# Eight of 22 feature tiles of the last down projection as seven block products, in three of its four output pairs

## The chip, the cores and the metric

The kernel runs on one core of one Trainium2 chip. The metric is the device time of one execution in microseconds (us): 1068.31, the median of three runs (1067.3 to 1068.74).

## What is computed

Two layers over 512 frames of 1024 features in float32. Layer 0 mixes tokens by latent attention, layer 1 by a gated short convolution, and each layer ends in the same feed-forward block; a last RMSNorm closes the trunk:

```python
for i in range(DEPTH):                                   # DEPTH = 2
    h = h + (mla_mixer if i % 2 == 0 else short_conv_mixer)(rms_norm(h, ...), ...)
    h = h + swiglu(rms_norm(h, ffn_norm[i]), ffn_w_gate[i], ffn_w_up[i], ffn_w_down[i])
return rms_norm(h, final_norm)

def swiglu(h, w_gate, w_up, w_down):                     # (512,1024) -> (512,2816) -> (512,1024)
    return (jax.nn.silu(h @ w_gate) * (h @ w_up)) @ w_down
```

The change is in the last product of all, `... @ w_down` of layer 1, and in the residual addition and norm behind it.

## The kernel before

Features lie on the 128 partitions, the 512 frames along the free dimension. So the residual stream is eight tiles of 128x512 (`xT`, "head" in the profile, since it shares that buffer), and the inner activations of the feed-forward block are 22 tiles (`inner`). A float32 product is made of three TensorE matmuls (lines 466 to 468): both operands are split into a high part rounded to `fp32r` and a rest, and high x high, high x rest and rest x high are added in a PSUM bank.

Weights stream in chunks through two slots. For each chunk the DMA queue loads `raw[s]`, ScalarE writes the high parts (`split`, L897), VectorE writes the rests (`split`, L1347), and then TensorE may read the slot. The semaphores are `raw_loaded`, `hi_split`, `w_split` and, when TensorE has read the last of a chunk, `chunk_done`; ScalarE waits for `chunk_done` before it overwrites the high parts. Each engine runs its own list in the written order. There is no scheduler: the order of the Python statements in the engine's block is the order on the engine.

The gate and up products use a seven-product block scheme, `winograd`: a pair of feature tiles and a pair of output tiles are taken as 2x2 blocks, and instead of eight block products there are seven, on 256 columns each, plus sums of blocks. The sums of the weights are made by VectorE in `forms` (four additions of 128x512) and split like a chunk (`forms_split`: 128x2048, then 128x1536 for the sums); the sums of the activations by `x_forms` (four subtractions of 128x256 for each pair of tiles). Between the products ScalarE copies partial sums out of the banks (L1173, L1180), and VectorE adds the four corners of the result.

The down projection is plain before the change. Eight output tiles are made in four pairs, and each pair takes its 22 feature tiles in three chunks, of 8, 8 and 6 tiles (`DOWN_K`). The first pair starts while the last inner tiles are still being split: ScalarE makes `inner_hi`, VectorE `inner_lo` (`inner_rests`, L1390), and TensorE waits for each tile by `operand_ready`. In `ffn` of VectorE the tail of this is: the rests of tiles 5 to 11, the split of the second weight chunk, the rests of tiles 12 to 21, and then, in `down_round`, the split of the third chunk. Of the last pair the second output tile is computed in two halves of 256 frames (`last_pair`), so that the norm can begin on the first half. Each finished tile is scaled by `rstd` and added to the residual (`add_scaled`), ScalarE squares it and VectorE adds the squares; `weigh` multiplies by the gains of the final norm, and the tail transposes, scales and stores.

`DOWN_AHEAD` gives the sizes of the chunks that are split ahead. `DOWN_BANKS` are the PSUM banks: (4, 5) and (6, 7); `HALF_BANKS` (7, 3) the two halves of the last tile.

## Time and profile before

| | |
|---|---|
| median of 3 runs | 1068.31 us |
| profiled execution, its own time | 1069.4 us |
| its span, first to last instruction | 1067.6 us |
| TensorE busy | 1057.6 us, 99% of the span |
| TensorE weight load busy | 956.1 us |
| VectorE busy | 806.5 us, 76% |
| ScalarE busy | 507.1 us, 48% |
| granted TensorE clock, mean | 1.000 |

A busy time is a sum over a whole engine. Matmuls overlap in the record: a 512-column matmul is listed with 0.39 us, but the next one starts 0.23 us later, so it is the distance from start to start that counts. "PEld" is the loading of the stationary operand, which overlaps too.

### The profile page before, as it was taken

What the parts mean: (1) busy time and instruction counts of PE and PEld (TensorE: products, weight loads), DVE (VectorE), ACT (ScalarE), POOL (GpSimd) and SP (SyncE); (2) the same over time, 40 slices, a digit from 0 to 9 for tenths busy, and PEclk for the clock granted to TensorE, in tenths of its full rate; (3) what the DMA queues carried; (4) which work ended last, traced back from release to release, by engine and by line L of the source; (5) the groups of instructions that cost most, each with busy time, mean ns of one, the idle gap of its engine ahead of it and who ended that gap; (6) DMA issues with size and microseconds to landing.
All of it is one profiled execution on the core that took longest, in us unless ns stands there. A gap on an engine that the chain in (4) does not pass through costs nothing.

```text
span 1067.6 us, 17579 instructions
## 1 busy us (share of the span) xinstructions
PE 1057.6 (99%) x6714; PEld 956.1 (90%) x6714; DVE 806.5 (76%) x1133; ACT 507.1 (48%) x720; POOL 40.5 (4%) x22
## 2 busy tenths in 40 slices
PE   9999999999999999999999999999999999999998
PEld 7788888889999999888888888888999999988887
DVE  5767774999999998734578677689999999873343
ACT  6586664745545555521353323365545554651221
POOL 0232221000000000000000000000000000000000
PEclk9999999999999999999999999999999999999999
DMA  7311121223233233233223232222333233222212
GB/s 270 116 63 40 56 79 45 114 99 103 113 118 115 82 117 108 80 108 108 93 95 107 91 115 83 91 107 80 118 118 112 87 115 118 97 91 108 99 40 80
DMA packets 16966, 106.21 MB, mean 99 GB/s; under 512 B 1888, under 2 KB 2272, under 8 KB 6432
## 3 DMA queue, kind: packets, MB, share of 16 engines
q1 hardware_dynamic: 16848, 105.43, 27.5%
q8 instruction: 25, 0.41, 0.2%
q0 software_dynamic: 80, 0.26, 0.1%
q14 instruction: 13, 0.11, 0.0%
HBM read 103.59 MB, written 2.10 MB: 99 GB/s over the span
## 4 chain that ended last, share of the span: by engine, by line
PE 91%; DVE 1%; ACT 1%; issue 1%; DVEq 0%
PE bank L466 30%; PE bank L468 29%; PE bank L467 29%; PE bank L613 1%; PE bank L627 1%; ACT split L1163 1%; DVE s_lo L1703 0%; PE bank L505 0%; PE bank L615 0%; PE bank L851 0%; PE bank L863 0%; DVE work L1692 0%; DVE raw L1690 0%; DVE sq L1397 0%; DVE work L1687 0%
## 5 line engine op out<-in xcount | busy, mean ns | idle before, releaser
L466 PE MATMUL bank<-x_hi,split 128*128 128x256 f32 (+1 forms) x704 | 204.4, 290 | 0.0
L467 PE MATMUL bank<-x_lo,split 128*128 128x256 f32 (+1 forms) x704 | 203.6, 289 | 0.0
L468 PE MATMUL bank<-x_hi,split 128*128 128x256 f32 (+1 forms) x704 | 203.6, 289 | 0.0
L897 ACT ACTIVATE split<-raw 128x2048 fp32r<-128x2048 f32 (+2 forms) x54 | 95.8, 1774 | 184.4 <-PE bank L468 180.4
L1347 DVE TENSOR_TENSOR split<-raw,split 128x2048 fp32r<-128x2048 f32 (+2 forms) x46 | 99.4, 2161 | 98.2 <-ACT split L897 98.1
L467 PE MATMUL bank<-inner_lo,split 128*128 128x512 f32 (+1 forms) x374 | 140.9, 377 | 0.0
L466 PE MATMUL bank<-inner_hi,split 128*128 128x512 f32 (+1 forms) x374 | 140.9, 377 | 0.0
L468 PE MATMUL bank<-inner_hi,split 128*128 128x512 f32 (+1 forms) x374 | 140.8, 376 | 0.0
L466 PE MATMUL bank<-x_hi,s_hi 128*128 128x256 f32 x480 | 134.4, 280 | 0.6 <-ACT work L1173 0.6
L467 PEld LDWEIGHTS bank<-x_lo,split 128*128 128x128 f32 x704 | 132.3, 188 | 3.0 <-issue 0.5
L466 PEld LDWEIGHTS bank<-x_hi,split 128*128 128x128 f32 x704 | 132.3, 188 | 3.0 <-issue 0.5
L468 PEld LDWEIGHTS bank<-x_hi,split 128*128 128x128 f32 x704 | 132.3, 188 | 2.5
L467 PE MATMUL bank<-x_lo,s_hi 128*128 128x256 f32 x480 | 134.0, 279 | 0.0
L468 PE MATMUL bank<-x_hi,s_lo 128*128 128x256 f32 x480 | 134.0, 279 | 0.0
L1697 DVE TENSOR_TENSOR split<-raw,split 128x2048 fp32r<-128x2048 f32 x44 | 100.8, 2290 | 14.8 <-ACT split L1163 13.2
L1163 ACT ACTIVATE split<-raw 128x2048 fp32r<-128x2048 f32 x44 | 84.3, 1915 | 43.0 <-DVE work L1692 42.9
L466 PE MATMUL bank<-a_hi,split 128*128 128x512 f32 (+1 forms) x264 | 100.9, 382 | 1.7 <-DVE split L1347 1.0
L468 PE MATMUL bank<-a_hi,split 128*128 128x512 f32 (+1 forms) x264 | 99.4, 377 | 0.0
L467 PE MATMUL bank<-a_lo,split 128*128 128x512 f32 (+1 forms) x264 | 99.4, 376 | 0.0
L1180 ACT ACTIVATE work<-bank 128x256 f32<-128x256 f32 x44 | 16.9, 385 | 164.0 <-PE bank L468 164.0
L466 PEld LDWEIGHTS bank<-x_hi,s_hi 128*128 128x128 f32 x480 | 90.2, 188 | 1.3 <-ACT work L1173 1.0
L467 PEld LDWEIGHTS bank<-x_lo,s_hi 128*128 128x128 f32 x480 | 90.2, 188 | 0.0
(240 smaller groups left out, 2087.3 us busy)
## 6 DMA issues: line engine op xcount, KB each, us to landing
raw<-weights_in SPq DMA_DIRECT2D x82, 1024.0 KB, 4.8
raw<-weights_in SPq DMA_DIRECT2D x12, 768.0 KB, 4.3
work<-x SPq DMA_DIRECT2D x4, 512.0 KB, 11.4
raw<-weights_in SPq DMA_DIRECT2D x4, 512.0 KB, 3.8
out<-head SPq DMA_DIRECT2D x3, 512.0 KB, 3.1
head<-head_in SPq DMA_DIRECT2D x1, 768.0 KB, 9.0
raw<-weights_in SPq DMA_DIRECT2D x3, 192.0 KB, 3.9
raw<-weights_in SPq DMA_DIRECT2D x1, 576.0 KB, 7.6
```

Of the source, the lines that this page charges most:

```text
L466: pe.matmul(o, lhs[0], rhs[0], start=start, stop=False, skip_group_check=True)
L467: pe.matmul(o, lhs[0], rhs[1], start=False, stop=False, skip_group_check=True)
L468: return pe.matmul(o, lhs[1], rhs[0], start=False, stop=stop, skip_group_check=True)
L613: pe.matmul(o, qr, key, start=False, stop=False, skip_group_check=True)
L627: tr = pe.transpose(bank[b][:, j * P:(j + 1) * P], work[:, p0:p0 + P], ident[:, :])
L897: act.activation(w_hi[s][:, 0:n], raw[s][:, 0:n], ACT.Copy).then_inc(hi_split[s], 1)
L1163: act.activation(block_hi[s][:, :], raw[s][:, :], ACT.Copy).then_inc(hi_split[s], 1)
L1180: act.activation(copies[g][0], bank[b][:, 0:HT], ACT.Copy).then_inc(drained[b], 1)
L1347: v.tensor_tensor(w_lo[s][:, 0:n], raw[s][:, 0:n], w_hi[s][:, 0:n], ALU.subtract).then_inc(w_split[s], 1)
L1697: v.tensor_tensor(block_lo[s][:, :], raw[s][:, :], block_hi[s][:, :], ALU.subtract).then_inc(w_split[s], 1)
```

## The change

1. The chunks of layer 1's down projection are cut 8, 6, 8 instead of 8, 8, 6 (`LAST_K`), and the pairs take them in the order of `LAST_ORDER`; the order of the loads (`LAST_N`) follows.
2. For output pairs 1, 2 and 3 the chunk of the last eight feature tiles (14 to 21) is computed by `winograd` from sums of the weights and of the activations. Pair 0 stays plain.
3. The sums of the activations are new work: `inner_forms` (VectorE, four subtractions of 128x256 for each of four pairs of tiles), their high parts (ScalarE) and their rests (`inner_tail_rest`). They are placed in the space of the gate and up operands, which are dead by then.
4. The block products end in banks 0 to 3 and not in the banks that hold the other 14 tiles' sum. So their corners are put together (`down_corners`), scaled and added to the residual on their own (`add_corners`), and the sum of the 14 tiles is added apart (`pair_sums`).
5. The last pair is ordered 8 tiles, block product, 6 tiles; within a chunk the whole tile is now done ahead of both halves (`last_pair`), and the second half uses bank 5 instead of 3.
6. ScalarE's load of the square-root table (`idle_sqrt`) moves from the middle of the projection to a place after the last copies of the last block product.

The core of the diff:

```diff
+LAST_K = [range(0, 8), range(8, 14), range(14, KF)]
+LAST_ORDER = [(0, 1, 2)] * 2 + [(0, 2, 1)] * 2
+LAST_N = [len(LAST_K[i]) * 2 * P for order in LAST_ORDER for i in order]
...
-LEFT_BANKS, HALF_BANKS = (4, 5, 7, 6), (7, 3)
+LEFT_BANKS, HALF_BANKS = (4, 5, 7, 6), (7, 5)
...
                 if last:
-                    for c in range(6):
-                        down_chunk(c)
-                    for c in range(3):
-                        down_chunk(c)
-                    for c in range(3, 6):
-                        last_pair(c)
+                    banks = DOWN_BANKS[0]
+                    chunk(0, banks, INNER, LAST_K[0], True, False, ready=made)
+                    chunk(1, banks, INNER, LAST_K[1], False, False, ready=made)
+                    last_tiles(0, banks, LAST_K[2], made)
+                    chunk(1, DOWN_BANKS[1], INNER, LAST_K[0], True, False)
+                    last_tiles(0, DOWN_BANKS[1], LAST_K[1])
+                    pe.wait_ge(inner_split, K_PAIRS)
+                    winograd(1, 0, inner_block, DOWN_SUMS)
+                    chunk(0, banks, INNER, LAST_K[0], True, False)
+                    winograd(1, 0, inner_block, DOWN_SUMS)
+                    last_tiles(0, banks, LAST_K[1])
+                    last_pair(1, DOWN_BANKS[1][0], LAST_K[0], False)
+                    winograd(0, 0, inner_block, DOWN_SUMS)
+                    last_pair(1, DOWN_BANKS[1][0], LAST_K[1], True)
...
+            def last_tiles(s, banks, ks, ready=None):
                 pe.wait_ge(w_split[s], T.add(f"slot{s}"))
+                for m, b in enumerate(banks):
                     for n, k in enumerate(ks):
+                        if ready is not None and m == 0:
+                            pe.wait_ge(operand_ready, ready + k + 1)
+                        mm = product(bank[b][:, :], slot(s, (n * 2 + m) * P), operand(INNER, k), False, n == len(ks) - 1)
+                    mm.then_inc((tile_summed, chunk_done[s])[m], 1)
...
+            def down_copies_of(s):                        # ScalarE
+                for n in (1, 5, 6):
+                    down_copy(n)
+                act.wait_ge(chunk_done[s], T.now(f"slot{s}"))
+                act.activation(down_copies["last"], bank[0][:, 0:HT], ACT.Copy).then_inc(drained[0], 1)
...
+            def inner_forms(k, m):                        # VectorE
+                (b11, b12), (b21, b22) = (tuple(half_of(tile(inner, m + i), h) for h in range(2)) for i in range(2))
+                t1, t2, t3, t4 = (inner_tail[:, k * 2 * SEQ + n * HT:k * 2 * SEQ + (n + 1) * HT] for n in range(4))
+                taken()
+                taken()
+                do(v.tensor_tensor(t1, b12, b11, ALU.subtract))
+                do(v.tensor_tensor(t3, b22, b12, ALU.subtract))
+                settle()
+                do(v.tensor_tensor(t2, b22, t1, ALU.subtract))
+                settle()
+                v.tensor_tensor(t4, b21, t2, ALU.subtract).then_inc(inner_formed, 1)
+                v.wait_ge(inner_formed, k + 1)
+                for i in range(m, m + 2):
+                    ready(lo(tile(inner_lo, i), tile(inner, i), tile(inner_hi, i)))
...
-                split(1)
-                inner_rests(range(12, KF))
+                split(1, DOWN_N[1] if name else LAST_N[1])
+                if name:
+                    inner_rests(range(12, KF))
+                else:
+                    inner_rests(range(12, LAST_K[2][0]))
+                    for k in range(K_PAIRS):
+                        inner_forms(k, LAST_K[2][2 * k])
...
+                def last_down():                          # VectorE
+                    split(0)
+                    split(1)
+                    for k in range(K_PAIRS):
+                        inner_tail_rest(k)
+                    pair_sums(DOWN_BANKS[0], (0, 1), 0, True)
+                    split(0, LAST_N[1])
+                    added()
+                    add_squares([tile(work, 4), tile(work, 5)])
+                    forms(1)
+                    forms_split(1, DOWN_SUMS)
+                    pair_sums(DOWN_BANKS[1], (2, 3), 0, False)
+                    settle()
+                    split(0)
+                    v.wait_ge(sums_split[1], T.now("sums1"))
+                    forms(1)
+                    down_corners(1)
+                    forms_split(1, DOWN_SUMS)
+                    add_corners((2, 3), True)
...
+                    down_corners(0)
+                    add_corners((KD - 2, KD - 1), False)
+                    settle()
+                    v.wait_ge(tile_summed, T.add("summed"))
+                    add_scaled(DOWN_BANKS[1][0], KD - 2)
```

Where it moves instructions. First VectorE, between the last gate and up products and the down projection; `split0` and `split1` are the weight slots, `inner_57` the inner tiles, and a row is one instruction (or several alike). Before, from the rests of tile 5 on:

```order
L1390 TENSOR_TENSOR inner_lo_58<-inner_57,inner_hi_59 128x512 [waits hi_taken,step]
L1390 TENSOR_TENSOR inner_lo_58<-inner_57,inner_hi_59 128x512 [waits hi_taken] x6
L1347 TENSOR_TENSOR split1<-raw1,split1 128x2048 [waits hi_split1]
L1390 TENSOR_TENSOR inner_lo_58<-inner_57,inner_hi_59 128x512 [waits hi_taken] x10
L1347 TENSOR_TENSOR split0<-raw0,split0 128x1536 [waits hi_split0]
L1347 TENSOR_TENSOR split1<-raw1,split1 128x2048 [waits hi_split1]
```

After, from the same place (the last rows are the first of four such groups):

```order
L1472 TENSOR_TENSOR inner_lo_58<-inner_57,inner_hi_59 128x512 [waits hi_taken,step]
L1472 TENSOR_TENSOR inner_lo_58<-inner_57,inner_hi_59 128x512 [waits hi_taken] x6
L1429 TENSOR_TENSOR split1<-raw1,split1 128x1536 [waits hi_split1]
L1472 TENSOR_TENSOR inner_lo_58<-inner_57,inner_hi_59 128x512 [waits hi_taken] x2
L1884 TENSOR_TENSOR inner_tail_80<-inner_57 128x256 [waits hi_taken]
L1885 TENSOR_TENSOR inner_tail_80<-inner_57 128x256
L1887 TENSOR_TENSOR inner_tail_80<-inner_57,inner_tail_80 128x256 [waits step]
L1889 TENSOR_TENSOR inner_tail_80<-inner_57,inner_tail_80 128x256 [waits step]
L1472 TENSOR_TENSOR inner_lo_58<-inner_57,inner_hi_59 128x512 [waits inner_formed]
L1472 TENSOR_TENSOR inner_lo_58<-inner_57,inner_hi_59 128x512
```

The rests of the last eight tiles are now made in four groups of two, each behind four subtractions. Second, VectorE from the fourth of these groups on, after:

```order
L1884 TENSOR_TENSOR inner_tail_80<-inner_57 128x256 [waits hi_taken]
L1885 TENSOR_TENSOR inner_tail_80<-inner_57 128x256
L1887 TENSOR_TENSOR inner_tail_80<-inner_57,inner_tail_80 128x256 [waits step]
L1889 TENSOR_TENSOR inner_tail_80<-inner_57,inner_tail_80 128x256 [waits step]
L1472 TENSOR_TENSOR inner_lo_58<-inner_57,inner_hi_59 128x512 [waits inner_formed]
L1472 TENSOR_TENSOR inner_lo_58<-inner_57,inner_hi_59 128x512
L1429 TENSOR_TENSOR split0<-raw0,split0 128x2048 [waits hi_split0]
L1429 TENSOR_TENSOR split1<-raw1,split1 128x2048 [waits hi_split1]
L1898 TENSOR_TENSOR inner_tail_lo_81<-inner_tail_80,inner_tail_hi_79 128x1024 [waits inner_tail_high] x4
L1942 TENSOR_TENSOR work<-bank4,rstd 128x512 [waits squares_added,tile_summed]
```

Only behind the fourth group stands the split of slot 0, which the third chunk of the first pair needs; before, it stood behind the plain rests. On TensorE the wait for it (`w_split0`) has moved ahead by two feature tiles, or 12 matmuls of 512 columns: it was at feature tile 16 and is at 14. Third, TensorE in the last output pair. Before, the whole tile (bank 6) and the two halves (banks 7 and 3) are interleaved:

```order
L466 MATMUL bank6<-inner_hi_59,split0 128x512
L467 MATMUL bank6<-inner_lo_58,split0 128x512
L468 MATMUL bank6<-inner_hi_59,split0 128x512
L466 MATMUL bank7<-inner_hi_59,split0 128x256
L467 MATMUL bank7<-inner_lo_58,split0 128x256
L468 MATMUL bank7<-inner_hi_59,split0 128x256
L466 MATMUL bank3<-inner_hi_59,split0 128x256
L467 MATMUL bank3<-inner_lo_58,split0 128x256
L468 MATMUL bank3<-inner_hi_59,split0 128x256
L466 MATMUL bank6<-inner_hi_59,split1 128x512 [waits w_split1]
```

After, the last half matmuls of the first chunk (bank 5) are followed by the block product in banks 0 to 3, which waits for these banks and for slot 0:

```order
L479 MATMUL bank5<-inner_hi_59,split1 128x256
L480 MATMUL bank5<-inner_lo_58,split1 128x256
L481 MATMUL bank5<-inner_hi_59,split1 128x256
L479 MATMUL bank0<-inner_hi_59,split0 128x256 [waits drained2,drained1,drained3,drained0,w_split0]
L480 MATMUL bank0<-inner_lo_58,split0 128x256
L481 MATMUL bank0<-inner_hi_59,split0 128x256
L479 MATMUL bank0<-inner_hi_59,split0 128x256
```

## Rows read from the trace of the kernel before

**Rows 1.** The page, busy time, share of the span, instructions of each engine.

```profile
PE 1057.6 (99%) x6714; PEld 956.1 (90%) x6714; DVE 806.5 (76%) x1133; ACT 507.1 (48%) x720; POOL 40.5 (4%) x22
```

**Rows 2.** The page, the chain that ended last, by engine.

```profile
PE 91%; DVE 1%; ACT 1%; issue 1%; DVEq 0%
```

**Rows 3.** Waits of TensorE: waited for, us in total, times, longest.

```profile
PE bank L466 <- DVE split L1347: 1.4, 2, 1.0
```

**Rows 4.** Busy time by engine in one stretch: PE, PEld, DVE, ACT, POOL.

```profile
966.00:1026.00 60.00, 60.00 (x266) 49.71 (x265) 20.64 (x18) 14.25 (x12) 0.00 (x0) 1.00 0.27 98
```

**Rows 5.** Timeline of TensorE in the down projection: start, duration, instruction.

```profile
936.27 0.40 PE L466 MATMUL bank<-inner_hi,split 128*128 128x512 f32 x1
...
1026.04 0.39 PE L466 MATMUL bank<-inner_hi,split 128*128 128x512 f32 x1
...
1048.53 0.40 PE L466 MATMUL bank<-inner_hi,split 128*128 128x512 f32 x1
...
1052.64 0.28 PE L466 MATMUL bank<-inner_hi,split 128*128 128x256 f32 x1
...
1056.83 0.28 PE L468 MATMUL bank<-inner_hi,split 128*128 128x256 f32 x1
```

**Rows 6.** Timeline of ScalarE: last copies of two consecutive block products.

```profile
916.93 0.38 ACT L1180 ACTIVATE work<-bank 128x256 f32<-128x256 f32 x1 [3.88 <-PE bank L468]
...
926.73 0.38 ACT L1180 ACTIVATE work<-bank 128x256 f32<-128x256 f32 x1 [3.88 <-PE bank L468]
```

**Rows 7.** Timeline of VectorE at the start of the down projection.

```profile
939.07 4.30 DVE L1390 TENSOR_TENSOR inner_lo<-inner,inner_hi 128x512 fp32r<-128x512 f32 x7
943.29 2.28 DVE L1347 TENSOR_TENSOR split<-raw,split 128x2048 fp32r<-128x2048 f32 x1
945.49 6.10 DVE L1390 TENSOR_TENSOR inner_lo<-inner,inner_hi 128x512 fp32r<-128x512 f32 x10
951.51 1.75 DVE L1347 TENSOR_TENSOR split<-raw,split 128x1536 fp32r<-128x1536 f32 x1
960.25 2.29 DVE L1347 TENSOR_TENSOR split<-raw,split 128x2048 fp32r<-128x2048 f32 x1 [6.99 <-ACT split L897]
```

**Rows 8.** Timeline of VectorE: four block subtractions of the convolution's operands, the next instruction.

```profile
554.68 0.42 DVE L1644 TENSOR_TENSOR conv_form<-conv_form 128x256 f32<-128x256 f32 x1
...
555.47 0.43 DVE L1647 TENSOR_TENSOR conv_form<-conv_form 128x256 f32<-128x256 f32 x1
555.93 0.42 DVE L1649 TENSOR_TENSOR conv_form<-conv_form 128x256 f32<-128x256 f32 x1
556.27 0.68 DVE L1687 TENSOR_TENSOR work<-raw 128x512 f32<-128x512 f32 x1
```

**Rows 9.** Timeline, VectorE and TensorE: the longest wait for a split.

```profile
21.98 2.29 DVE L1347 TENSOR_TENSOR split<-raw,split 128x2048 fp32r<-128x2048 f32 x1 [2.38 <-ACT split L897]
...
24.32 0.50 PE L466 MATMUL bank<-a_hi,split 128*128 128x512 f32 x1 [0.95 <-DVE split L1347]
```

**Rows 10.** Timeline of ScalarE at the start of the down projection.

```profile
942.27 5.31 ACT L911 ACTIVATE inner_hi<-inner 128x512 fp32r<-128x512 f32 x10
...
958.30 1.92 ACT L897 ACTIVATE split<-raw 128x2048 fp32r<-128x2048 f32 x1 [9.34 <-PE bank L468]
```

**Rows 11.** Timeline of TensorE: its last matmuls.

```profile
1061.49 1.04 PE L872 MATMUL bank<-ident,raw 128*128 128x128 f32 x8
```

**Rows 12.** Stretches at the end: PE busy, granted clock (here 0.20 us each).

```profile
1066.60:1066.80 0.20, 0.00 (x0) 1.00 0.09 31
1066.80:1067.00 0.20, 0.00 (x0) 0.55 0.00 0
```

**Rows 13.** Stretches at the start: PE busy and its matmuls (x), granted clock.

```profile
2.00:3.00 1.00, 1.00 (x7) 1.00 0.88 151
...
5.00:6.00 1.00, 1.00 (x10) 1.00 0.79 228
```

**Rows 14.** Timeline of VectorE: the scaling of the last whole tile.

```profile
1052.84 0.69 DVE L1612 TENSOR_TENSOR work<-bank,rstd 128x512 f32<-128x512 f32 x1 [11.10 <-PE bank L468]
```

More of the change, by code:

```diff
@@ new lines, in whole, with half, last_pair @@
+            def whole(s, b, n, k):
+                return product(bank[b][:, :], slot(s, n * 2 * P), operand(INNER, k), k == 0, False)
+            def half(s, h, n, k):
+                return product(bank[HALF_BANKS[h]][:, 0:HT], slot(s, (n * 2 + 1) * P),
+                               tuple(half_of(t, h) for t in operand(INNER, k)), k == 0, False)
+            def last_pair(s, b, ks, ends):
+                pe.wait_ge(w_split[s], T.add(f"slot{s}"))
+                if ks[0] == 0:
+                    open_bank(b)
@@ new lines, in pair_sums @@
+            def pair_sums(banks, ms, s, final):
+                for b, m in zip(banks, ms):
+                    if b == banks[0]:
+                        v.wait_ge(tile_summed, T.add("summed"))
+                    else:
+                        done(s)
+                    t = tile(work, 4 + b % 2)
+                    v.wait_ge(squares_added, T.now("added"))
+                    drain(b, v.tensor_tensor(t, bank[b][:, :], rstd[:, :], ALU.mult))
+                    landed(b)
+                    add_to_x(t, m, final)
@@ L1829, in down_round @@
                             add_scaled(banks[0], ms[0])
-                            if last and pair == 1:
-                                added()
-                                weigh([ms[0]])
-                                add_squares([tile(work, 4)])
-                            if last and pair == 1:
-                                continue
                             done(c % 2)
@@ L1838, in down_round @@
                             next_operands(ms, name)
-                        if not (last and c >= 4):
-                            split(c % 2, DOWN_AHEAD[c])
-                        if name and m:
+                        split(c % 2, DOWN_AHEAD[c])
+                        if m:
                             conv_operands(c)
-                        if last and c in (2, 3):
-                            v.wait_ge(w_split[c % 2], T.now(f"slot{c % 2}"))
-                        if last and c == 2:
-                            weigh(range(KD // 2))
@@ L1847, in down_round, with last_down @@
-                        if last and c == 3:
-                            weigh(range(KD // 2, KD - 2))
-                down_round(0, False)
-                down_round(4, not name)
+                def last_down():
+                    split(0)
+                    split(1)
+                    for k in range(K_PAIRS):
+                        inner_tail_rest(k)
+                    pair_sums(DOWN_BANKS[0], (0, 1), 0, True)
+                    split(0, LAST_N[1])
+                    added()
[3 more added lines that the diff above has]
+                    pair_sums(DOWN_BANKS[1], (2, 3), 0, False)
+                    settle()
+                    split(0)
+                    v.wait_ge(sums_split[1], T.now("sums1"))
[3 more added lines that the diff above has]
+                    add_corners((2, 3), True)
+                    added()
+                    add_squares([tile(work, 4), tile(work, 5)])
+                    split(0, LAST_N[1])
+                    down_corners(1)
+                    split(1)
+                    add_corners((4, 5), False)
+                    settle()
+                    forms(0)
+                    pair_sums(DOWN_BANKS[0], (4, 5), 0, True)
+                    forms_split(0, DOWN_SUMS)
+                    added()
+                    add_squares([tile(work, 4), tile(work, 5)])
+                    v.wait_ge(w_split[0], T.now("slot0"))
+                    v.wait_ge(sums_split[0], T.now("sums0"))
+                    weigh(range(KD // 2))
+                    split(1, LAST_N[1])
+                    v.wait_ge(w_split[1], T.now("slot1"))
+                    weigh(range(KD // 2, KD - 2))
+                    down_corners(0)
+                    add_corners((KD - 2, KD - 1), False)
+                    settle()
+                    v.wait_ge(tile_summed, T.add("summed"))
+                    add_scaled(DOWN_BANKS[1][0], KD - 2)
+                    added()
+                    weigh([KD - 2])
+                    add_squares([tile(work, 4)])
@@ L2016, in weight_stream @@
         for m in range(KD // 2):
-            for ks in DOWN_K:
-                yield columns(w["ffn_w_down"][layer][ks[0] * P:(ks[-1] + 1) * P], span(m * 2 * P))
+            for i in LAST_ORDER[m] if layer else range(3):
+                ks = (LAST_K if layer else DOWN_K)[i]
+                chunk = columns(w["ffn_w_down"][layer][ks[0] * P:(ks[-1] + 1) * P], span(m * 2 * P))
+                yield block_order(chunk) if layer and m and i == 2 else chunk
 def kernel(**inputs):
```

140 lines of the change are left out of this document (101 added, 39 removed).

## The prediction, made before the changed kernel had run

> **What bounds the kernel now.** I read the page first. TensorE is busy in 99% of the span [rows 1], and the chain that ended last lies on it for 91% [rows 2]. The waits come next: in the whole execution TensorE waits for a weight split for 1.4 us [rows 3]. In its middle TensorE is busy without a break for 60 us while VectorE works 20.6 us and ScalarE 14.3 us of them [rows 4]. So what counts there is the number of matmuls and their distance from start to start, and whatever makes TensorE wait is added in full. The start of this stage is different. There VectorE works without a break from 939.07 to 953.26 [rows 7], since TensorE has begun the projection at 936.27 [rows 5] while the rests of the inner tiles are still being made.
>
> **What TensorE saves.** A 512-column matmul costs the distance of its start to the next. Three output pairs are 3 x 132 = 396 of them, from 936.27 to 1026.04 [rows 5]: 0.2267 us each. A block product is 84 matmuls of 256 columns. Two that follow each other directly end 926.73 - 916.93 = 9.80 us apart [rows 6], 0.1167 each. It replaces 8 tiles x 2 outputs x 3 = 48 long matmuls, 10.88 us. That is 1.08 us less in each of pairs 1 and 2, together 2.16.
> In the last pair, before: from 1026.04 to the last start at 1056.83 plus one step of 0.12, 30.91 us [rows 5]. After: 42 long ones for the whole tile, at (1052.64 - 1048.53) / 18 = 0.228 us, 9.59; 84 half matmuls at (1056.83 - 1052.64) / 35 = 0.120 us, 10.06; and the block product, 9.80. The sum is 29.45, so 1.46 less. It is more than 1.08 because here the block product replaces 24 long matmuls and 48 halves, and two halves take longer than one long matmul (0.24 against 0.227). All in all TensorE has 2.16 + 1.46 = 3.62 us less to do.
> Bounds: with the inner tiles as operands the 252 matmuls of the block products could run at the 0.120 us of the halves, not at 0.1167. That would take back 0.8 us. I see nothing that would make them faster than 0.1167.
>
> **What VectorE gets to do at the start.** TensorE is through with feature tiles 0 to 13 of the first pair after 84 matmuls, at 936.27 + 19.04 = 955.31. Then it needs the split of slot 0. Before, the same slot was split at 951.51 to 953.26 [rows 7] and needed two tiles later, at 936.27 + 96 x 0.2267 = 958.03: 4.8 us of cover.
> Now the list of VectorE, step by step. The seven rests end where the next row starts, 943.29. The split of slot 1 is 1536 wide now: 1.75 us long, and the next one starts 0.08 earlier than its end, as the 2.28 us split was followed after 2.20 [rows 7]. So 944.96. Two plain rests, at (951.51 - 945.49) / 10 = 0.60 each: 946.16. Now four groups. The four subtractions are the same shape, with the same two waits for its own results, as those of the convolution's operands: the fourth starts 1.25 us after the first, and an instruction that waits for its predecessor starts 0.46 us after it [rows 8]. The first rest of a group waits for the fourth subtraction. So a group is 1.25 + 0.46 + 2 x 0.60 = 2.91 us, and four are 11.64: 957.80. Then the split of slot 0, 2048 wide, 2.28: it ends at 960.08.
> ScalarE isn't late: its ten high parts end at about 947.6 [rows 10], even 0.43 us earlier with the shorter split ahead of them, and the high half of slot 0 takes 1.92 us [rows 10] after the first chunk is done at 936.27 + 10.88 = 947.15. The load of that chunk has had the slot since before 931. The rests themselves come in time: tiles 14 and 15 at 949, tiles 20 and 21 at 958, while TensorE would want tile 20 at 955.3 + 6 x 0.68 = 959.4.
> So TensorE, ready at 955.31, waits for VectorE till 960.08. After the longest such wait in the trace it started 0.05 us behind the end of the split, with a first matmul longer by 0.1 [rows 9, 5]. I take 4.9 us. Bounds: 4.4, if the settles cost nothing (each is worth about 0.1 [rows 8]), and 5.3, if the waits between engines inside the groups cost 0.1 us each.
> What queues behind that split: the split of slot 1 (960.1 to 962.3), needed only at the start of pair 1, 10.9 us after the restart; and four rests of the sums, needed by the first block product 19 us later. No second wait follows from this one.
>
> **The rest of the projection.** Each block product adds on VectorE four additions of 0.69 [rows 8], a 1536-wide rest of 1.75 [rows 7] and some six shorter instructions, about 7 us, and on ScalarE about 3 us. In 28.8 us of a pair VectorE was working 10 [rows 4], so it has room, but its order could still make TensorE wait. The tightest place: slot 1 is free for new high parts when the chunk ahead is done, 8.2 us before the block product. ScalarE's 1.92 and VectorE's 2.28 with two handovers leave 3.7 us of cover, and the sums, at 1.75 more, are wanted 1.4 us later. In the last pair VectorE comes to the block's rests behind `add_corners`, `forms` and `pair_sums`; by the same durations it is done some 4 us ahead. Cost 0 at these places; if one cover is gone, its excess is paid in full.
>
> **The end.** Before, VectorE was idle for 11.1 us when the last whole tile was summed, and started at 1052.84 [rows 14]. Now the corners of the last block product stand in front of it, with 4.1 us (18 long matmuls) to be done in: a copy with its handovers 0.7, two additions of 0.45, two scalings and two additions at 0.60 to 0.72. That is 4.3 us against 4.3 including the handover. I take 0; bounds 0 and +0.4. The moved table load stands where ScalarE idles.
>
> **Sum.** 4.9 - 3.6 = +1.3 us against the profiled execution (span 1067.6, own time 1069.4). The median of the runs is 1.1 below that own time, and the difference applies to both: 1068.31 + 1.3 = 1069.6. A measurement of this kernel can tell about 0.2%, 2.1 us, from no change, so this is "the same", by a hair's width on the slow side.
>
> **Rivals.**
> (a) The clock falls in the wait (slower). TensorE would be idle for about 4.7 us. At the end of the kernel its last matmuls end at 1062.5 [rows 11], and the granted clock stands at 0.55 in 1066.80 to 1067.00 [rows 12]: it has gone down to 1.2 GHz about 4.3 us after the last work. The new wait is a little longer than that. Against it: one fall doesn't tell that the next comes as soon, and the other waits here are too short to say. At 1.2 GHz 512 columns take 0.427 us, not 0.227. How long that lasts is bounded by the start of the kernel, where TensorE ran 7 matmuls in one us at 2 and 10 at 5 [rows 13], so it came to its pace about 4 us after its first at 1.1; the clock's own record says 1.00 there, which speaks against this reading. The cost is 0 to 1.9 us (half of 3.9), I take 1.4: 1071.0. Once the wait is above some 4.3 us the clock decides whether this is a loss that can be measured.
> The Trainium skill (TensorE: Matmul & The Clock Gate, "HAM oscillation — how this bites in real kernels") says that a TensorE kept waiting between two groups of matmuls is throttled again and starts the next group cold. By that rule this rival is the rule and my forecast the exception; the trace has its one fall at the end, after 4.3 us, and no restart behind it.
> (b) The wait doesn't come, or is small (faster). If VectorE reached the split by 955.3, TensorE would keep all 3.6 us: 1064.7. It decides at a wait of 3.6 us, so VectorE would have to be 1.3 us ahead of my times for zero. For it: TensorE's list could have slack if the groups overlapped with something. Against it: VectorE alone runs these steps, they are gapless in the trace, and each duration is from the same shapes.
> (c) Another wait later, at the block's rests or at the end (above): about +1, 1070.6. For it: VectorE has more, in a fixed order; against it: covers of 3.7 and 4 us.
> (d) The change doesn't do what it says, so that the block products give nothing: they would have to run at 0.13 us a matmul, and neither the block products of the gate and up stage [rows 6] nor the halves do. I give it no chance of its own beyond the bound of 0.8.
>
> **Chances.** Forecast 0.55 (1069.6, own range 1068.6 to 1070.8), (a) 0.28, (b) 0.10, (c) 0.07. Faster by over 0.2% (below 1066.2) needs (b): 0.09. Slower by over 0.2% (above 1070.4): most of (a), most of (c) and the upper end of the forecast: 0.31. The rest is the same, 0.60. The range reaches into (a) and (c) but leaves (b) out: 1067.6 to 1071.8.
>
> **What would show it.** TensorE idle once, for 4.4 to 5.0 us, released by VectorE's 2048-wide split, at about 960 us; no other wait of TensorE over 0.3 us in the projection; block products 9.8 us long; the whole tile and halves of the last pair at 0.228 and 0.120. A granted clock below 1.00 in the 3 us after the restart is rival (a), and long matmuls 0.4 us apart with it. Wrong would be a wait under 3.6 us, or a wait at `w_split` or `sums_split` in pairs 1 to 3.

## Result: 0.44% slower, 1072.4 us

| | before | after |
|---|---|---|
| median of the runs, same chips | 1067.3 us (9) | 1072.4 us (9) |
| ratio to before, 95% interval | | 1.0044, 1.0032 to 1.0056 |
| profiled execution, its span | 1067.6 us | 1071.7 us |
| first matmul of the down projection | 936.27 | 936.04 |
| from there to the first norm matmul, "the stage" | 120.84 us | 124.64 us |
| first norm matmul to the end of the span | 10.5 us | 11.0 us |
| granted TensorE clock, mean | 1.000 | 0.996 |

The forecast was 1069.6 with a range up to 1071.8; the time is above the range. The forecast started from the median of the first three runs of before, 1068.31; by the median of nine, 1067.3, the change cost 5.1 us where +1.3 was forecast. The ratio is worth +4.7 us (3.4 to 6.0), the two spans differ by 4.1. I call the time from the first matmul of the down projection to the first matmul of the norm's sums "the stage". Where it starts changes by some us from execution to execution of any kernel, so profiles are compared by the stage's length.

The page of the changed kernel, busy time, share, instructions [rows 1]; the chain by engine [rows 2]; and the longest wait of TensorE for a weight split, total, times, longest [rows 3]:

```profile
PE 1057.9 (99%) x6798; PEld 960.8 (90%) x6798; DVE 843.0 (79%) x1192; ACT 519.1 (48%) x739; POOL 40.5 (4%) x22
```

```profile
PE 89%; DVE 3%; ACT 1%; issue 1%; DVEq 0%; ACTq 0%
```

```profile
PE bank L479 <- DVE split L1429: 4.9, 2, 4.7
```

TensorE was to have 3.6 us less work, and its busy time is 0.3 us up, with a wait of 4.7 us on top. Busy time doesn't tell more matmuls from slower ones; the clock does. The windows around the wait, in the columns of [rows 4] (PE, PEld, DVE, ACT, POOL, clock, DMA share and GB/s):

```profile
955.00:960.00 5.00, 0.33 (x3) 0.04 (x1) 4.90 (x8) 4.62 (x4) 0.00 (x0) 0.74 0.00 0
960.00:965.00 5.00, 5.00 (x13) 3.97 (x14) 5.00 (x4) 1.08 (x2) 0.00 (x0) 0.58 0.76 261
957.40:957.60 0.20, 0.00 (x0) 0.00 (x0) 0.20 (x1) 0.20 (x1) 0.00 (x0) 0.50 0.00 0
964.20:964.40 0.20, 0.20 (x2) 0.16 (x2) 0.20 (x2) 0.00 (x0) 0.00 (x0) 0.99 0.88 369
966.00:1026.00 60.00, 60.00 (x347) 53.07 (x346) 34.13 (x41) 18.31 (x20) 0.00 (x0) 1.00 0.24 86
```

Read them in order of time. In the wait the clock goes to 0.50, which is 1.2 GHz, at 957.4. It is back at 964.2, and TensorE gets 13 matmuls into the 5 us behind 960, where 22 would fit at 0.227. The last row answers to [rows 4]: TensorE is busy all the time there, so from 966 to 1026 there is no second wait (and none from there to the end of the stage), though VectorE works 34.1 us of the 60 instead of 20.6.

TensorE's timeline (start, duration), answering to [rows 5]:

```profile
954.90 0.39 PE L481 MATMUL bank<-inner_hi,split 128*128 128x512 f32 x1
959.96 0.80 PE L479 MATMUL bank<-inner_hi,split 128*128 128x512 f32 x1 [4.67 <-DVE split L1429]
960.56 0.63 PE L480 MATMUL bank<-inner_lo,split 128*128 128x512 f32 x1
...
963.97 0.51 PE L479 MATMUL bank<-inner_hi,split 128*128 128x512 f32 x1
964.31 0.39 PE L480 MATMUL bank<-inner_lo,split 128*128 128x512 f32 x1
...
992.00 0.28 PE L479 MATMUL bank<-inner_hi,split 128*128 128x256 f32 x1
...
1001.92 0.40 PE L479 MATMUL bank<-inner_hi,split 128*128 128x512 f32 x1
...
1056.14 0.28 PE L479 MATMUL bank<-inner_hi,split 128*128 128x256 f32 x1
...
1060.33 0.28 PE L481 MATMUL bank<-inner_hi,split 128*128 128x256 f32 x1
1060.68 0.35 PE L883 MATMUL bank<-ones,acc 128*128 128x1 f32 x2
```

The matmul due at 954.90 + 0.23 = 955.13 starts at 959.96: 4.83 us. (The profile puts the wait at 4.67 us, since it counts from the end of the record before, and it is this figure that the table of the experiments gives.) The next ones are 0.43 us apart (963.97 - 960.56 = 3.41 us for 8 steps), then 0.23 again. A block product is 1001.92 - 992.00 = 9.92 us.

VectorE's timeline, answering to [rows 7]:

```profile
943.07 1.75 DVE L1429 TENSOR_TENSOR split<-raw,split 128x1536 fp32r<-128x1536 f32 x1
...
945.94 0.42 DVE L1884 TENSOR_TENSOR inner_tail<-inner 128x256 f32<-128x256 f32 x1
...
947.19 0.42 DVE L1889 TENSOR_TENSOR inner_tail<-inner,inner_tail 128x256 f32<-128x256 f32 x1
947.65 1.30 DVE L1472 TENSOR_TENSOR inner_lo<-inner,inner_hi 128x512 fp32r<-128x512 f32 x2
948.86 0.42 DVE L1884 TENSOR_TENSOR inner_tail<-inner 128x256 f32<-128x256 f32 x1
...
957.62 4.49 DVE L1429 TENSOR_TENSOR split<-raw,split 128x2048 fp32r<-128x2048 f32 x2
```

The group from 945.94 to 948.86 is 2.92 us, the fourth subtraction 1.25 behind the first, and the split of slot 0 starts at 957.62. The last row is two splits of 2.24 us in one.

### The profile page after: what moved, and what is told of

It reads as the page before. It is cut to its first block, busy times and chain, and to the rows that moved or that the text cites. A ratio compares the mean times of both kernels' runs of the same rounds, so it can differ in the third digit from the quotient of the medians.

```text
span 1071.7 us, 17823 instructions
## 1 busy us (share of the span) xinstructions
PE 1057.9 (99%) x6798; PEld 960.8 (90%) x6798; DVE 843.0 (79%) x1192; ACT 519.1 (48%) x739; POOL 40.5 (4%) x22
## 4 chain that ended last, share of the span: by engine, by line
PE 89%; DVE 3%; ACT 1%; issue 1%; DVEq 0%; ACTq 0%
PE bank L479 29%; PE bank L480 29%; PE bank L481 29%; PE bank L626 1%; PE bank L640 1%; DVE inner_lo L1472 1%; ACT split L1190 1%; DVE s_lo L1782 0%; DVE split L1429 0%; PE bank L518 0%; PE bank L628 0%; PE bank L883 0%; PE bank L895 0%; DVE inner_tail L1889 0%; DVE inner_tail L1887 0%
## 5 line engine op out<-in xcount | busy, mean ns | idle before, releaser
L929 ACT ACTIVATE split<-raw 128x2048 fp32r<-128x2048 f32 (+2 forms) x51 | 90.1, 1766 | 144.5 <-PE bank L481 141.1
L1429 DVE TENSOR_TENSOR split<-raw,split 128x2048 fp32r<-128x2048 f32 (+2 forms) x43 | 92.5, 2152 | 60.2 <-ACT split L929 60.1
L479 PE MATMUL bank<-inner_hi,split 128*128 128x512 f32 (+1 forms) x342 | 128.5, 376 | 4.7 <-DVE split L1429 4.7
L481 PE MATMUL bank<-inner_hi,split 128*128 128x512 f32 (+1 forms) x342 | 128.2, 375 | 0.0
L480 PE MATMUL bank<-inner_lo,split 128*128 128x512 f32 (+1 forms) x342 | 128.2, 375 | 0.0
L1779 DVE TENSOR_TENSOR split<-raw,split 128x2048 fp32r<-128x2048 f32 x47 | 107.6, 2290 | 21.8 <-ACT split L1190 20.9
L1190 ACT ACTIVATE split<-raw 128x2048 fp32r<-128x2048 f32 x47 | 90.0, 1916 | 59.0 <-DVE work L1774 50.4
```

Source lines behind the costliest of these rows:

```text
L479: pe.matmul(o, lhs[0], rhs[0], start=start, stop=False, skip_group_check=True)
L480: pe.matmul(o, lhs[0], rhs[1], start=False, stop=False, skip_group_check=True)
L481: return pe.matmul(o, lhs[1], rhs[0], start=False, stop=stop, skip_group_check=True)
L929: act.activation(w_hi[s][:, 0:n], raw[s][:, 0:n], ACT.Copy).then_inc(hi_split[s], 1)
L1190: act.activation(block_hi[s][:, :], raw[s][:, :], ACT.Copy).then_inc(hi_split[s], 1)
L1429: v.tensor_tensor(w_lo[s][:, 0:n], raw[s][:, 0:n], w_hi[s][:, 0:n], ALU.subtract).then_inc(w_split[s], 1)
```

## Experiments

Fifteen runs followed, of ten new kernels and of the changed kernel once more. "Stage" is the stage's length in the profile (before 120.84, after 124.64), "wait" the longest wait of TensorE in it.

| kernel | ratio, 95% | median us (runs) | stage | wait | slow clock behind it |
|---|---|---|---|---|---|
| after | 1.0044, 1.0032 to 1.0056 | 1072.4 (9) | 124.64 | 4.7 | yes |
| after_again | | 1073.0 (1) | 124.60 | 4.7 | yes |
| filler20 | 1.0022, 1.0012 to 1.0031 | 1070.0 (9) | 122.64 | 0.15 | no |
| filler10 | 1.0039, 1.0026 to 1.0053 | 1072.7 (9) | 122.66 | 2.4 | no |
| filler10_again | | 1071.1 (1) | 124.27 | 2.4 | yes |
| split_after_3 | 0.9994, 0.9983 to 1.0005 | 1067.2 (11) | 119.74 | 1.7 | no |
| split_after_1 | 0.9981, 0.9970 to 0.9991 | 1066.5 (11) | 118.28 | 0.3 | no |
| left_banks | 0.9978, 0.9969 to 0.9988 | 1065.3 (12) | 118.26 | 0.3 | no |
| best | 0.9981, 0.9969 to 0.9992 | 1065.0 (9) | 117.66 | none | no |
| best_pad_timed | 0.9965, 0.9952 to 0.9979 | 1064.1 (5) | 117.66 | none | no |
| forms_alone | 1.0035, 1.0022 to 1.0048 | 1071.4 (7) | 123.11 | 1.9 | no |
| forms_again | | 1070.5 (1) | 124.72 | 2.0 | yes |
| forms_again2 | | 1070.9 (1) | 123.13 | 2.0 | no |
| forms_filler8 | 1.0016, 1.0007 to 1.0025 | 1069.6 (12) | 123.14 | filled | no |
| before_pad | | 1067.6 (1) | 120.91 | none | no |
| best_pad | | 1067.1 (1) | 117.65 | none | no |

Each ratio is to runs of the kernel before on the same chip. Where it is empty, the kernel ran once, with a profile. The medians come from several chips, so compare the ratios and not the medians. best_pad_timed is best_pad's kernel, and forms_again, forms_again2 and filler10_again are those of forms_alone and filler10.

**The wait taken away by order.** The edit in VectorE's list; split_after_3 has `k == 2`.

```diff
                     for k in range(K_PAIRS):
                         inner_forms(k, LAST_K[2][2 * k])
+                        if k == 0:
+                            split(0)
...
                 def last_down():
-                    split(0)
                     split(1)
```

> The changed kernel, with VectorE's split of slot 0 for the third chunk made behind the first of the four groups (tiles 14 and 15) instead of behind the fourth. Theory (the wait of 4.7 us and the clock that fell in it cost some 7.0 us together, the block products save 3.4): the split ends at about 951, ahead of 955.1, no wait of TensorE over 0.3 us is left in the projection, the clock stays at 1.00, and the time is 1067.3 - 3.4 = 1063.9, ratio 0.9968. Rival (the loss comes from the block products, the longer list of VectorE or the end): the wait goes, but the time stays at or above 1068.

> The changed kernel, with the split of slot 0 behind the third group. The split ends at about 957.1, so TensorE waits 1.9 to 2.0 us. If so short a wait leaves the clock alone: 1067.3 + 1.9 - 3.4 = 1065.8, ratio 0.9986. If the clock falls in it too (in the profile of the changed kernel it stood at 0.50 only 2.2 us after the last matmul): 1.5 to 2.2 us more, 1067.3 to 1068.0, ratio 1.0000 to 1.0007.

Measured: 0.9981 (forecast 0.9968) and 0.9994 (forecast 0.9986, or 1.0000 and more with a fall of the clock). Both gained less than forecast: the stage is 2.56 and 1.10 us shorter than before, not 3.4 and 1.5, and behind it 0.5 us are lost that were forecast at nothing (see the end, below). In split_after_3 the wait of 1.7 us left the clock at 1.00 in its profile. In split_after_1 VectorE's split of slot 0 comes at 951.36 and TensorE has one small wait, for the rests of feature tile 20:

```profile
951.36 2.29 DVE L1429 TENSOR_TENSOR split<-raw,split 128x2048 fp32r<-128x2048 f32 x1 [0.21 <-ACT split L929]
```

```profile
961.86 0.50 PE L479 MATMUL bank<-inner_hi,split 128*128 128x512 f32 x1 [0.31 <-DVE inner_lo L1472]
```

All work of the change is still there, in another order, and the stage is 6.4 us shorter than in after. So the loss is the wait and what hangs on it, and the saving of the block products is real.

**The clock without the wait.** Twenty matmuls that nothing reads keep TensorE busy in the gap, so the third chunk starts when VectorE is done, as in after, with the clock up.

```diff
+                    taken(7)
+                    for _ in range(20):
+                        pe.matmul(bank[7][:, :], inner_hi[:, 0:P], tile(inner_hi, 0), start=True, stop=True, skip_group_check=True)
                     last_tiles(0, banks, LAST_K[2], made)
```

> The changed kernel, with 20 extra 512-column matmuls (their result is never read) on TensorE in front of the third chunk, so that it computes for 20 x 0.227 = 4.5 us of the 4.8 us in which it would wait. Theory (the clock's fall costs 2.2 us beside the wait): the third chunk still starts at about 960, the clock stays at 1.00, the 48 matmuls behind it run 0.227 us apart, and the time is 1067.3 + 4.8 - 3.4 + 0.1 = 1068.8, ratio 1.0014, with runs as close together as those of before (2.2 us). Rival (the clock costs nothing of note and the excess over my forecast is somewhere else): the time stays at 1071.5 to 1072.5.

The timeline and one window of filler20:

```profile
953.25 4.70 PE L840 MATMUL bank<-inner_hi 128*128 128x512 f32 x20
958.10 0.50 PE L479 MATMUL bank<-inner_hi,split 128*128 128x512 f32 x1 [0.15 <-DVE split L1432]
```

```profile
958.00:965.00 7.00, 6.90 (x30) 5.74 (x31) 7.00 (x7) 1.24 (x2) 0.00 (x0) 1.00 0.73 265
```

TensorE makes more matmuls and the kernel is faster than after. The clock stays at 1.00, and the stage is 124.64 - 122.64 = 2.00 us shorter, with the third chunk starting as late as in after (23.9 us behind the start of the stage in both). By the runs it is 1.0044 against 1.0022, 2.3 us. That is the price of the slow clock: rival (a), shown by itself. The forecast of 1.0014 was low, since it took the saving of the block products at 3.4 us and the end at 0.1. after_again, the changed kernel in a second execution, had the same wait and the same fall, and the mean clock is 0.996 or 0.997 in all nine runs of after, against 0.998 to 1.000 in filler20's.

> The changed kernel once more, for a second look at its clock. If the fall belongs to the wait: a wait of 4.7 us with a fall inside it, and 1.5 to 3.5 us lost in the matmuls behind it. From the first inner matmul to the first norm matmul 123.8 to 126 us (124.64 in the first profile, 122.64 with 20 extra matmuls and no fall). If it was an accident of one execution: about 122.5.

**How short a wait is enough.** filler10 is filler20 with 10 matmuls, so 2.4 us of the wait stay. forms_alone is the kernel before with only the new subtractions, whose wait is 1.9 to 2.0 us (`inner_forms` is defined as in the change):

```diff
-                inner_rests(range(12, KF))
+                if name:
+                    inner_rests(range(12, KF))
+                else:
+                    inner_rests(range(12, 14))
+                    for k in range(K_PAIRS):
+                        inner_forms(k, 14 + 2 * k)
```

forms_filler8 adds 8 of the filler matmuls to it, ahead of the third chunk.

> The changed kernel with 10 extra matmuls instead of 20, so that TensorE is idle for about 2.4 us and not 4.7. Same start of the third chunk, so only the clock can differ. If the clock falls only in waits longer than about 4 us: as with 20, ratio 1.0022. If it also falls in a wait of 2.4 us: up to 2 us more, ratio 1.003 to 1.004, and a mean clock of 0.998 or less in most runs.

> The kernel before, with one part of the change alone: VectorE makes the sixteen subtractions of 128x256 among the rests of tiles 14 to 21, and nothing reads them; chunks, matmuls and all else stay. By my steps VectorE's split of slot 0 ends 6.8 us later, at 960.1, and TensorE needs it at 958.0: a wait of 2.1 us. Without a fall of the clock 1069.4, ratio 1.0020; with one 1071.0 to 1071.6, ratio 1.0035 to 1.004. Rival (the subtractions are hidden by waits of VectorE for other engines): 1067.3, ratio 1.000.

> The kernel before with the sixteen subtractions alone, and 8 extra matmuls (1.8 us) in the 2.1 us in which TensorE would wait. The subtractions alone measured 1.0035 though in their profile the wait was 1.94 us and the clock stayed up (2.3 us, 1.0021). If the missing 1.4 us are falls of the clock in the other runs: 1067.5 + 2.3 = 1069.8, ratio 1.0021. Rival (they are something else that the subtractions cost): 1.0035 stays.

The first profiles of filler10 and forms_alone showed no fall, yet filler10's runs gave 1.0039 where filler20's, with a stage as long, gave 1.0022, and forms_alone's gave 1.0035 where its stage of +2.3 us is worth 1.0021, and with the filler 1.0016. So both kernels ran again, as they were.

> The kernel before with the sixteen subtractions alone, once more. Its first profile had a wait of 1.94 us and no fall of the clock, but its runs have a mean clock of 0.9979 against 0.9996 of before and took 1.2 us more than that profile explains. If short waits lower the clock in some executions: here or in the next one a stretch at 0.50 behind the wait, and 1 to 2 us more than 123.1 us from the first inner matmul to the first norm matmul. Rival (the low clock of the other runs lies elsewhere, as at the end): 123.1 again.

> As the run before this, a third look: a fall behind the wait of 1.9 us with 1 to 2 us lost, or 123.1 us again.

> The changed kernel with 10 extra matmuls and an idle time of 2.4 us, a second look. Its first profile had no fall (122.66 us from the first inner to the first norm matmul). If idle times of about 2 us lower the clock in some executions, it may fall here: 123.5 to 125 us. If only the wait of 4.7 us does: 122.6 again.

Two executions of forms_alone's kernel, with the same wait. TensorE and its windows in the first (forms_again), then in the second (forms_again2):

```profile
957.62 0.50 PE L468 MATMUL bank<-inner_hi,split 128*128 128x512 f32 x1 [1.97 <-DVE split L1349]
957.95 0.40 PE L469 MATMUL bank<-inner_lo,split 128*128 128x512 f32 x1
...
958.47 0.63 PE L468 MATMUL bank<-inner_hi,split 128*128 128x512 f32 x1
...
961.83 0.39 PE L470 MATMUL bank<-inner_hi,split 128*128 128x512 f32 x1
```

```profile
958.30:961.70 3.40, 3.40 (x10) 2.64 (x9) 1.68 (x1) 0.00 (x0) 0.00 (x0) 0.51 0.87 279
```

```profile
959.41 0.50 PE L468 MATMUL bank<-inner_hi,split 128*128 128x512 f32 x1 [1.98 <-DVE split L1349]
```

```profile
960.00:963.40 3.40, 3.40 (x17) 2.79 (x15) 1.76 (x1) 0.00 (x0) 0.00 (x0) 1.00 0.78 274
```

In the first, TensorE is at work again, with two matmuls at full pace, and then the clock falls: 10 matmuls in the 3.4 us in which the second has 17. It costs 124.72 - 123.13 = 1.6 us of the stage. filler10_again did the same behind its 2.4 us (124.27 against 122.66). So a wait of 2 us can cost the clock and need not. How often isn't settled: three profiles of forms_alone's kernel and two of filler10's, one fall in each. That falls make up the excess of forms_alone fits: its mean clock is 0.998 or 0.997 in six of seven runs, and 0.999 or 1.000 in all twelve of forms_filler8. It was not counted, and the mean clock can't count it: split_after_3's profile has 0.998 too, with its one fall at the kernel's end, behind the last matmul. For filler10 falls can be a part at most. Its mean clock is 0.999 in six of nine runs, and its first profile, without a fall, is of an execution of 1074.3 us, one of its slowest: the stage started at 938.85 there, so what it had too much lies ahead of the stage. The intervals of filler10 and filler20 overlap, and filler10's excess stays open.

**The rest of the gain, and the end.** left_banks is split_after_1 with the banks of the tail's transposes in another order; best also lets both tiles of the pair take each feature tile of the third chunk together, so that tile 20 is wanted later.

```diff
-LEFT_BANKS, HALF_BANKS = (4, 5, 7, 6), (7, 5)
+LEFT_BANKS, HALF_BANKS = (4, 7, 5, 6), (7, 5)
...
-                    last_tiles(0, banks, LAST_K[2], made)
+                    pe.wait_ge(w_split[0], T.add("slot0"))
+                    for n, k in enumerate(LAST_K[2]):
+                        pe.wait_ge(operand_ready, made + k + 1)
+                        for m, b in enumerate(banks):
+                            mm = product(bank[b][:, :], slot(0, (n * 2 + m) * P), operand(INNER, k), False, n == len(LAST_K[2]) - 1)
...
```

> The split behind the first group, and the turned left halves of token blocks 1 and 2 in banks 7 and 5 instead of 5 and 7. In the four changed kernels profiled so far VectorE scales the left half of block 1 4.15 us after the first norm matmul, and in the kernel before 3.79; its store leaves later and the last stores land 10.95 to 11.02 us after that matmul instead of 10.5. Theory (bank 5, which now takes the last half of the last tile, is what delays it): 3.79 again, the end 0.3 to 0.5 us earlier than with the split alone (ratio 0.9977 against 0.9981, too small for the runs, to be read in the profile). Rival (the delay has nothing to do with the bank): 4.15 stays.

> The split behind the first group, the banks of left_banks, and the third chunk of the first pair takes both output tiles for each feature tile in turn, so that it needs tiles 18 to 21 later. With the split alone TensorE still waited 0.5 us for tile 20 (a gap of 0.70 and one of 0.34 instead of two of 0.23). Theory: no gap over 0.3 us in the projection, so 0.6 us less, and 0.4 less at the end: from the first inner matmul to the first norm matmul 117.7 us (118.28 with the split alone, 120.84 before), time 1067.5 - 3.1 - 0.0 = 1064.4 to 1065, ratio 0.997 to 0.9975.

best has no wait left and the shortest stage, 117.66 us as forecast, 3.18 us under before; its ratio of 0.9981 missed the forecast of 0.9970 to 0.9975 by the end, which stayed at 11.0 us. The banks were my theory for a loss at the end, and it fell. In every changed kernel the tail behind the first norm matmul takes 11.0 us, before 10.5, and the place where they part is VectorE's second output row. Before, after, and best, each the reciprocal and the row it scales:

```profile
1060.62 0.17 DVE L1949 RECIPROCAL numbers<-numbers 128x2 f32<-128x2 f32 x1 [0.26 <-ACT numbers L1290]
1060.90 0.75 DVE L1955 TENSOR_SCALAR head<-bank,numbers 128x512 f32<-128x512 f32 x1
```

```profile
1064.19 0.17 DVE L2139 RECIPROCAL numbers<-numbers 128x2 f32<-128x2 f32 x1 [0.26 <-ACT numbers L1372]
1064.83 0.75 DVE L2145 TENSOR_SCALAR head<-bank,numbers 128x512 f32<-128x512 f32 x1 [0.47 <-PE bank L904]
```

```profile
1055.44 0.17 DVE L2146 RECIPROCAL numbers<-numbers 128x2 f32<-128x2 f32 x1 [0.26 <-ACT numbers L1378]
1056.07 0.75 DVE L2152 TENSOR_SCALAR head<-bank,numbers 128x512 f32<-128x512 f32 x1 [0.47 <-PE bank L910]
```

The distance is 0.28 us before and 0.64 and 0.63 in the changed ones, with other banks too (left_banks: 0.63). The reciprocals stand 3.51 us behind the first norm matmul in all three. The store that waits for this row is issued 0.36 us later (4.92 us behind that matmul, before 4.56). VectorE's next rows start at 5.10 and the last two stores are issued from 6.26 in all three, yet they land 0.5 us later; how the late store does that no trace shows. Is it the length of VectorE's list? before_pad adds 60 one-column memsets to the kernel before, 20 of them behind each of three chunks of the last projection, and best_pad 12 to best. The second edit:

```diff
                     add_corners((2, 3), True)
+                    for _ in range(12):
+                        small(v.memset(numbers[:, 38:39], 0.0))
```

> The kernel before, with 60 one-column memsets of an unused cell in VectorE's idle times of the last down projection, so that VectorE's list is about as long as in the changed kernel (59 more rows). Nothing waits for them. Theory (the 0.36 us that VectorE's second output row comes late in all changed kernels belongs to the place in its longer list, not to what the change computes): the row starts 4.15 us after the first norm matmul instead of 3.79, and the last stores end 10.8 to 11.0 us after it instead of 10.3 to 10.6. Rival (it comes from the banks or the order of the changed kernel): 3.79 stays.

> The kernel with the split behind the first group, tiles in turn and swapped banks, with 12 such memsets more in an idle time of VectorE. If the late row belongs to a place in the list, 12 rows more move it: 3.79 us after the first norm matmul, or a gap of about 0.4 us between two other rows of the end. If it belongs to the changed kernel's work: 4.14 stays. From the first inner to the first norm matmul 117.7 us as without them.

> The same kernel as the run before, timed. From the profiles: 3.2 us less from the first inner to the first norm matmul, and the end as long as before (10.3 us, not 11.0), so 1067.4 - 3.2 = 1064.2, ratio 0.9970. Without the shift of VectorE's list it measured 0.9981 (0.9969 to 0.9992), with 0.5 us more at the end in its profile. If the late row costs nothing in the runs: 0.998 again.

VectorE in best_pad:

```profile
1058.51 0.17 DVE L2148 RECIPROCAL numbers<-numbers 128x2 f32<-128x2 f32 x1 [0.26 <-ACT numbers L1378]
1058.78 0.75 DVE L2154 TENSOR_SCALAR head<-bank,numbers 128x512 f32<-128x512 f32 x1
```

Twelve more instructions, and the row is back at 0.27; before_pad never lost it (0.27, one run at 1067.6 us). So it isn't the length of the list, and not what the change computes either. That it is the place in the list at which the instruction stands fits, but isn't shown: two paddings are few, and they may act in another way. What the engine does in these 0.36 us no trace shows; I leave it open. Timed, best_pad is 0.9965, 1064.1 us: faster than both kernels. Its interval overlaps that of best, so that the padding itself helps rests on the profiles (10.3 us behind the first norm matmul in both, 11.0 in the nine of the changed kernels without it).

## Why the prediction was wrong

**The step that failed** is the one on the clock: "(a) The clock falls in the wait", given 0.28 while the forecast without it had 0.55. The wait was forecast at 4.9 us, and the prediction itself said that above some 4.3 us the clock decides. So the sum has the clock at nothing, and it should have had +2.0. The reason given was "one fall doesn't tell that the next comes as soon". The 4.3 us were read from the end of the kernel [rows 11, 12]. In the new wait the last matmul's record ends at 955.29 and the clock is down at 957.4: 2.1 us. The Trainium skill (TensorE: Matmul & The Clock Gate, "HAM oscillation — how this bites in real kernels") has the next group of matmuls start cold behind such a wait. I quoted it and called my forecast the exception; both profiles of this kernel agree with the page. The price was mis-sized too: 1.4 taken with a top of 1.9, and 2.0 measured, since the clock stays low for 4.2 us behind the restart. Its bound had been read from the start of the kernel, where the record has the clock at 1.00 [rows 13]. And the other waits were called too short to say; forms_again shows that a wait of 2.0 us can be enough.

That one fall doesn't tell when the next comes is true, and it cuts the other way: at the ends of the 17 profiles of this case the clock falls 2.2 to 5.1 us behind the last matmul, and in 16 of them the delay is shorter than the wait that was forecast. The two extremes, each the last matmuls and the stretch (0.20 us) in which the clock has fallen, split_after_3 (last record ends at 1061.02) and filler20 (1062.27):

```profile
1059.98 1.04 PE L904 MATMUL bank<-ident,raw 128*128 128x128 f32 x8
1063.20:1063.40 0.20, 0.00 (x0) 0.00 (x0) 0.00 (x0) 0.00 (x0) 0.00 (x0) 0.50 0.97 369
```

```profile
1061.23 1.04 PE L907 MATMUL bank<-ident,raw 128*128 128x128 f32 x8
1067.40:1067.60 0.20, 0.00 (x0) 0.00 (x0) 0.00 (x0) 0.00 (x0) 0.00 (x0) 0.53 0.00 0
```

The other steps, as terms of the sum, in us of the profile:

| term | predicted | measured |
|---|---|---|
| wait for the split of slot 0 | +4.9 (4.4 to 5.3) | +4.83 |
| TensorE's saving | -3.62 (-2.8 at the least) | -3.0; -3.18 in best, without a wait |
| clock | 0 (rival: +1.4) | +2.0 |
| rest of the projection | 0 | 0 |
| end | 0 (to +0.4) | +0.5 |
| sum | +1.3 | +4.3 |

- **The wait** came out as worked, step by step: groups of 2.92 (forecast 2.91), the split of slot 0 from 957.62 (957.80), one wait of TensorE at that place and none later. The way, one engine's list added up from like shapes, held.
- **The saving** was 0.4 to 0.6 too large. Three block products of 9.92 instead of 9.80 are 0.36 of it: 0.118 us a matmul, between my 0.1167 and the bound of 0.120. Another 0.07 is the step behind the last half matmul, 0.35 instead of 0.28. In after the first step behind the restart, 0.60 where the next ones are 0.43, is the other 0.17; the prediction had 0.1 of this in the wait.
- **Rival (b)**, no wait, was built in best: 3.18 of its 3.6 us came. **Rival (c)** did not come: TensorE has no wait in pairs 1 to 3.
- **The end** was sought at the wrong place. VectorE takes up the last whole tile at 1056.41 (below), 0.27 us after TensorE has begun the halves at 1056.14; before, it was 0.20 us [rows 5, 14]. So the corners in front of it cost no more than 0.07. The 0.5 us come 8 us later, in the norm's tail, where the change adds no work.

```profile
1056.41 0.69 DVE L1694 TENSOR_TENSOR work<-bank,rstd 128x512 f32<-128x512 f32 x1
```

- **The range** ended at 1071.8. Rival (a) at 1071.0 with the upper bounds of two other terms (0.8 of the saving, 0.4 of the end) would have been 1072.2, near the measured 1072.4. I let the bounds of single terms stand only around the forecast and not around the rival.

The sum of 4.3 stands against 4.7 (3.4 to 6.0) by the runs and 4.1 by the spans, where this execution started the stage 0.2 us early. The prediction's +1.3 is below the interval.

## What to carry to other kernels

A new wait of an engine that is otherwise never idle can cost more than its length, in slow matmuls behind it: here 4.8 us of wait brought 2.0 us of slow matmuls, and once 2.0 us brought 1.6. So put the work that another engine gets behind the split that is due first (one moved line turned +0.44% into -0.19%), and if a wait can't be moved, try work that nothing reads in its place (it gave back 2.3 us).

When a rival and the forecast differ by one threshold that is known from a single event, that event is no safe limit (here 4.3 us, and the next falls 2.1 and 2.1): give the rival at least even odds, and stack the other terms' bounds on it when setting the range.

## What the runs showed of the hardware

- TensorE's granted clock fell to 0.50 at 2.1 us behind the last matmul's record in the new wait (after and after_again). At the kernel's end it fell 4.3 us behind it in before [rows 11, 12], and 2.2 to 5.1 us behind it over the 17 profiles. Behind waits of 2.0 and 2.4 us it fell only 0.7 to 1.3 us after TensorE had started again, in some executions of a kernel and not in others. The row from filler10_again that shows the step from 0.23 to 0.43 us, 1.6 us behind the restart at 957.96:

```profile
959.59 0.63 PE L479 MATMUL bank<-inner_hi,split 128*128 128x512 f32 x1
```

- In filler20 twenty matmuls with no reader, 4.7 us in a free bank, kept the clock at 1.00.
- The same VectorE instruction, with its producers done as early, starts 0.28 us behind its predecessor in before and 0.63 in best, and 0.27 with twelve small instructions put ahead of it in best's list (0.27 and 0.28 in the two profiles). Where it is late, the last two stores land 3.8 us after their issue (after, best); where it isn't, 3.3 (before) or 3.1 (before_pad, best_pad).
